# First attention: scores copied out of PSUM with their minimum, scores two units ahead of the transposes, and a buffer for the weighed maps

## The reference

```python
def diff_attn_core(q, k, v, lam):
    s = jnp.einsum('bqhcd,bkhcd->bhcqk', q.astype(jnp.float32), k.astype(jnp.float32))
    p = jax.nn.softmax(s * (1.0 / math.sqrt(HEAD_DIM)), axis=-1)
    a = p[:, :, 0] - lam * p[:, :, 1]
    return jnp.einsum('bhqk,bkhe->bqhe', a.astype(v.dtype), v)
```

## Time and profile before

| | us |
|---|---|
| median of 3 runs | 3198.42 |
| lowest and highest run | 3198.42, 3210.07 |
| the profiled execution | 3200.17 |
| its span in the trace | 3198.4 |
| TensorE (PE) busy, share | 3010.0, 94% |
| VectorE (DVE) busy, share | 1422.7, 44% |
| ScalarE (ACT) busy, share | 902.1, 28% |
| GpSimd (POOL) busy, share | 261.9, 8% |

### The profile page before, as it was taken

The page is one execution under the profiler, slowest core; times in us unless marked ns, Lnnn a source line. Parts: engine busy times, 40 slices in busy tenths (PEclk is TensorE's granted clock), DMA queues, the critical chain, the costliest instruction groups (busy, mean ns, idle before and its releaser), DMA issues. The chain is left out here.

```text
span 3198.4 us, 38018 instructions
## 1 busy us (share of the span) xinstructions
PE 3010.0 (94%) x15018; PEld 2314.2 (72%) x15018; DVE 1422.7 (44%) x2219; ACT 902.1 (28%) x1422; POOL 261.9 (8%) x278
## 2 busy tenths in 40 slices
PE   6999999899978999999999999999999988989995
PEld 4888888777734677887888888888888765764442
DVE  3646463545566466465333343333342268521113
ACT  3211121242155232223222232322233355321111
POOL 1000000001100000001000011000010145012221
PEclk8999999999989899999999999999999989989997
DMA  6323333221000166463223211223232300438995
GB/s 238 123 97 120 108 114 126 69 86 53 27 1 1 53 225 233 152 238 101 92 92 105 84 61 66 92 95 102 81 120 92 112 27 1 169 121 340 362 368 203
DMA packets 78062, 395.79 MB, mean 124 GB/s; under 512 B 17521, under 2 KB 19953, under 8 KB 51313
## 3 DMA queue, kind: packets, MB, share of 16 engines
q1 hardware_dynamic: 66416, 385.65, 32.9%
q0 software_dynamic: 11520, 8.43, 0.9%
HBM read 444.34 MB, written 16.78 MB: 144 GB/s over the span
## 5 line engine op out<-in xcount | busy, mean ns | idle before, releaser
L676 PE MATMUL ps<-h_high_ffn,weights_high_ffn 128*128 128x512 f32 (+1 forms) x1696 | 624.6, 368 | 8.4 <-issue 3.8
L677 PE MATMUL ps<-h_low_ffn,weights_high_ffn 128*128 128x512 f32 (+1 forms) x1696 | 623.5, 368 | 0.0
L678 PE MATMUL ps<-h_high_ffn,weights_low_ffn 128*128 128x512 f32 (+1 forms) x1696 | 623.0, 367 | 0.0
L676 PEld LDWEIGHTS ps<-h_high_ffn,weights_high_ffn 128*128 128x128 f32 x1696 | 320.0, 189 | 63.8 <-issue 9.2
L678 PEld LDWEIGHTS ps<-h_high_ffn,weights_low_ffn 128*128 128x128 f32 x1696 | 320.1, 189 | 53.1
L677 PEld LDWEIGHTS ps<-h_low_ffn,weights_high_ffn 128*128 128x128 f32 x1696 | 320.3, 189 | 52.7
L676 PE MATMUL ps<-hidden_high_ffn,weights_high_ffn 128*128 128x512 f32 (+1 forms) x880 | 328.2, 373 | 19.3 <-DVE weights_low_ffn L811 12.0
L760 ACT ACTIVATE weights_high_ffn<-weights 128x2048 fp32r<-128x2048 f32 (+4 forms) x160 | 243.8, 1524 | 346.6 <-PE ps L678 275.6
L811 DVE TENSOR_TENSOR weights_low_ffn<-weights,weights_high_ffn 128x2048 fp32r<-128x2048 f32 (+4 forms) x160 | 289.6, 1810 | 84.7 <-ACT weights_high_ffn L760 83.2
L677 PE MATMUL ps<-hidden_low_ffn,weights_high_ffn 128*128 128x512 f32 (+1 forms) x880 | 326.8, 371 | 0.0
L678 PE MATMUL ps<-hidden_high_ffn,weights_low_ffn 128*128 128x512 f32 (+1 forms) x880 | 326.4, 371 | 0.0
(11 more groups left out here) (438 smaller groups left out, 4563.3 us busy)
## 6 DMA issues: line engine op xcount, KB each, us to landing
weights<-in_ffn_gu SPq DMA_DIRECT2D x88, 1024.0 KB, 5.0
big<-in_w_exp_gu SPq DMA_DIRECT2D x32, 2048.0 KB, 13.0
scratch_ffn<-in_w_mod SPq DMA_DIRECT2D x35, 1536.0 KB, 6.6
weights<-in_ffn_d SPq DMA_DIRECT2D x24, 768.0 KB, 4.3
weights<-in_w_in SPq DMA_DIRECT2D x16, 1024.0 KB, 4.9
weights<-in_ffn_d SPq DMA_DIRECT2D x24, 640.0 KB, 3.9
weights<-in_w_exp_dn SPq DMA_DIRECT2D x15, 1024.0 KB, 18.4
hbuf<-in_w_exp_dn SPq DMA_DIRECT2D x12, 1024.0 KB, 19.2
```

What stands on the lines that cost most here:

```text
L676: pe.matmul(out, wh, xh, start=(k == 0), stop=False)
L677: pe.matmul(out, wh, xl, start=False, stop=False)
L678: mm = pe.matmul(out, wl, xh, start=False, stop=(k == n - 1))
```

## The change

Four things. The maximum becomes a `tensor_tensor_reduce`, which reads the scores from PSUM, adds a column of zeros, multiplies by -1, writes the result to `first_prob` in SBUF and takes its minimum; the exponential then reads SBUF, in place, with a scale of -1. The scores of a unit wait for this instruction of the unit before and no longer for the exponentials. TensorE's scores run two units ahead of the transposes, VectorE's copies one unit ahead of the weighing, and ScalarE copies the transposes of u - 2 before the exponentials of u. The weighed sum goes to a buffer of its own, `first_weighed` (two of 3 KB per partition), in place of `first_prob`. The sums of squares move from unit 1 to unit 3 of a head, and the output copy goes behind the weighing.

```diff
+        weighed = [placed(f"first_weighed{b}", (24 + 4 * b) * K1, [P, NT]) for b in range(2)]
@@ TensorE
                     if u > 0:
-                        pe.wait_ge(fm["exp"].sem, 2 * u)
+                        pe.wait_ge(fm["top"].sem, 2 * u)
...
-                        mm = pe.transpose(tp[:, m * P:(m + 1) * P], pr[u % 2][:, 0, m * P:(m + 1) * P], ident[:])
+                        mm = pe.transpose(tp[:, m * P:(m + 1) * P], weighed[u % 2][:, m * P:(m + 1) * P], ident[:])
...
                 scores(0)
+                scores(1)
                 for u in range(tiles):
-                    if u + 1 < tiles:
-                        scores(u + 1)
+                    if u + 2 < tiles:
+                        scores(u + 2)
                     turn(u)
                     if u >= QT and u % QT < 3:
                         values_product(u // QT - 1, u % QT)
-                    if u >= 2 * QT and u % QT == 1:
+                    if u >= 2 * QT and u % QT == 3:
                         out_sums(u // QT - 2)
@@ ScalarE
                 for u in range(tiles):
                     if u >= 2:
-                        scalar.wait_ge(fm["turned"].sem, u - 1)
+                        evacuate(u - 2)
                     for c in range(2):
                         scalar.wait_ge(fm["top"].sem, 2 * u + c + 1)
-                        scalar.activation(pr[u % 2][:, c, :], sc[:, c, 0:NT], ACT.Exp, bias=top[:, u % 2, c:c + 1],
+                        scalar.activation(pr[u % 2][:, c, :], pr[u % 2][:, c, :], ACT.Exp, bias=top[:, u % 2, c:c + 1], scale=-1.0,
                                           accum_out=total[:, c, u:u + 1]).then_inc(fm["exp"].sem, 1)
-                    if u > 0:
-                        evacuate(u - 1)
...
+                evacuate(tiles - 2)
                 evacuate(tiles - 1)
@@ VectorE
-                for u in range(tiles):
+                def negated(u):
                     for c in range(2):
                         vector.wait_ge(fm["scores"].sem, 2 * u + c + 1)
                         if u >= 2:
                             vector.wait_ge(fm["exp"].sem, 2 * (u - 2) + c + 1)
-                        vector.reduce_max(top[:, u % 2, c:c + 1], sc[:, c, 0:NT], AX_X, negate=True)\
-                            .then_inc(fm["top"].sem, 1)
-                    if u >= QT and u % QT == 3:
-                        output(u // QT - 1)
+                            vector.wait_ge(fm["differences"].sem, u - 1)
+                        vector.tensor_tensor_reduce(pr[u % 2][:, c, :], sc[:, c, 0:NT], column[:, 0:1].to_broadcast([P, NT]), -1.0, 3e38,
+                                                    ALU.add, ALU.min, top[:, u % 2, c:c + 1]).then_inc(fm["top"].sem, 1)
+
+                vector.wait_ge(fm["column"].sem, 2)
+                negated(0)
+                for u in range(tiles):
+                    if u + 1 < tiles:
+                        negated(u + 1)
                     vector.wait_ge(fm["exp"].sem, 2 * u + 2)
...
+                    if u >= 2:
+                        vector.wait_ge(fm["turned"].sem, u - 1)
-                    vector.scalar_tensor_tensor(pr[u % 2][:, 0, :], pr[u % 2][:, 1, :], weight, pr[u % 2][:, 0, :],
+                    vector.scalar_tensor_tensor(weighed[u % 2], pr[u % 2][:, 1, :], weight, pr[u % 2][:, 0, :],
                                                 ALU.mult, ALU.add).then_inc(fm["differences"].sem, 1)
+                    if u >= QT and u % QT == 3:
+                        output(u // QT - 1)
```

## The result

| | us |
|---|---|
| changed kernel, median of 4 runs | 3164.51 (3156.84 to 3172.84) |
| kernel before, median of 4 runs | 3198.42 (3195.23 to 3210.07) |
| ratio, 95% interval | 0.9889 (0.9869 to 0.9909) |
| profiled execution of the changed kernel, its span | 3165.37, 3163.6 |
| profiled execution of before, its span | 3200.17, 3198.4 |

The change makes the kernel 1.1% faster (0.9 to 1.3% by the interval): 34.8 us between the profiled executions, 33.9 between the medians, for 33.2 in the sum of the prediction. Three windows of the profile after (columns as in the earlier trace rows) are heads 1 to 7 from unit 5 to the last scores, the last values, and the first head with the start of unit 4.

A forecast was written before the change was run, and what follows sets the result against it. It took a loop of waits (scores, maxima, exponentials, next scores; 4.55 us) to bound the kernel's first attention. Gains of 3.8 (first head), 27.3 (units 4 to 31) and 2.1 (tail), 33.2 in all, took 3200.17 to 3167 us; range 3158 to 3190.

The forecast's parts named there:

- The loop: First attention: the next scores wait only for the copies of the unit before, 3.44 us a loop, formerly 4.55.
- TensorE bounds with values: Heads 1 to 7: TensorE's own work sets the pace in the three value units of each head, 4.04 us each.
- The new instruction: VectorE's negated copy of 768 score columns takes 0.90 us, 1.80 a unit, as the maxima did.
- Rival 2: Heads 1 to 7: VectorE or the loop bounds, at 1.22 us a copy and 4.15 a unit; 3176 us, chance 0.11.
- Order and buffer: Transposes go behind scores u+2, with a buffer of their own: no new wait, as weighing ends 1.5 us after the copies.
- The exponential out of SBUF: ScalarE's exponentials reading SBUF cost some 0.04 us more each, 0.07 a unit, beside 1.2 us of slack.
- The first head: Units 0 to 4: 22.62 us shrink to 18.6 to 18.9, scores 1 and 2 at half clock; gain 3.8.
- The clock: Heads 1 to 7: TensorE runs at 2.4 GHz throughout, where the granted clock averaged 0.93 before.
- rivals 1 and 4: Rival 1: the clock dips as now, 14% of the time at half; 3178 us, chance 0.13. Rival 4 has its own line.
- rival 4: Heads 1 to 7 slower: half clock 40% of the time breaks even, from 63% kernel 0.5% worse; 75% gives 3233; chance 0.05.
- The tail: Last first maximum to last values loses 1.0 us; last values at full clock gain 3.1; net gain 2.1.
- rival 3: Whole kernel: no change, the gain given back by later transfers or the clock elsewhere; 3197 us, chance 0.09.

The follow-up runs named there:

- the two loads: Changed kernel with an extra 256-column VectorE addition, or two extra small TensorE matmuls, in units with values: 27 periods in 105.59 and 116.6 us.
- the TensorE load: Changed kernel with two useless 128-column matmuls behind the values in every unit that carries them: 27 periods in 116.6 us, units of 4.60.
- the split on GpSimd: Changed kernel with the low half of w_o's first slab made by GpSimd instead of VectorE: unit 0 to unit 4 in 20.3 us for 15.8.
- the fillers: Kernel before with useless small matmuls in TensorE's gaps: stage 181.9 us for 190.6, ratio 0.9995 (0.9979 to 1.0011).

## Why the prediction was right

**The loop.** Forecast 1.59 + 1.80 + 0.05 = 3.44, measured 3.49. That its release decides is shown by the wait put back (5.09 in every kind of unit).

**TensorE bounds with values.** Forecast 4.04 from the rows of one unit, measured 4.02; shown by the two loads. A head takes 3 x 4.02 + 3.49 = 15.55, forecast 15.6. The sum over units 4 to 31 came out 0.8 us above the forecast (105.6 for 104.8) for one reason: the forecast took full clock throughout, and one group of scores ran at half (1.4 us).

**The new instruction.** Forecast 0.90, measured 0.88 from start to start, accumulator read hidden: the extrapolation from 256 and 512 columns (0.87) was the better row, and the operand of stride zero adds nothing that shows. Rival 2 fell.

**Order and buffer.** Priced at no new wait, and none came: the transposes start 1.49 us behind the scores, 1.50 before. The 0.33 us of idle in their row was 0.35 before and is that of the weight loads: the matmuls of the scores fill it (939.88 + 1.56 = 941.44, the transposes start at 941.37). So the prediction read a third of a microsecond of idle into TensorE's 1.50 that is hardly there, and its sign of being wrong, transposes that wait more than 0.3 us, was set below a value that the old kernel had too. The sum, taken from start to start, isn't touched. What the kernel would lose without them was not in the prediction; it is 17 us each by their experiments.

**The exponential out of SBUF** takes 924 ns instead of 897 for the 768 columns:

```profile
L1450 ACT ACTIVATE first_prob<-first_prob,top 128x768 f32<-128x768 f32 x64 | 58.9, 924 | 7.7 <-DVE top L1502 7.7
```

27 ns are less than the 35 between the two functions of the earlier trace rows. They are also less than the 43 ns estimated from the page of the Trainium skill that the prediction cites (VectorE: DVE Perf Modes, "The TRN2 errata — SBUF-src ops pay a fixed extra latency per instruction"). It is off the path either way.

**The first head was mis-sized:** 3.8 forecast, 6.8 measured. The step that failed is the assumption that scores 1 and 2 run at half clock, as scores 0 and 1 did before. They ran at full clock (units of 3.49). The execution with the TensorE load, whose edit does not touch this head, shows the other case: units of 4.86, 4.86, 3.49, 5.35, 18.56 us in all, which is the forecast 18.6. Nor does the idling just before decide it: after the same 1.93 us of it, scores 2 ran at full clock in the changed kernel and at half with the split on GpSimd:

```profile
883.58 1.56 PE L1337 MATMUL ps<-K,Q 64*128 64x512 f32 x8 [1.93 <-DVE top L1502]
...
885.67 2.93 PE L1337 MATMUL ps<-K,Q 64*128 64x512 f32 x8 [1.93 <-DVE top L1508]
```

Of the seven executions that share these units four had them at full clock. So this term is 3.8 or 6.8 from execution to execution, and the 3 us above the forecast are the luck of the one that was profiled.

**The clock.** Full in heads 1 to 7, as taken, but for one group of scores (895.91); rivals 1 and 4 fell. Of the 35.2 us of the stage's gain the dips explain some 9 to 10, by the fillers in the kernel before. Of the 26.5 between unit 4 and unit 31 the dips are 5.9 (132.1 to 126.2), and the 20.6 from there to 105.6 are the change itself, with the old loop at 4.57 us at full clock; 4.8 of them hang on the move of the sums, by the run with the sums put back. In rival 4 the 63% and the 40% are not of one kind: by its own formula heads 1 to 7 alone cost the 16 us from some 59% on.

**The tail** came out at -1.0 and +2.9. The second depends on the profile of before that is taken: by the other two it is 3.0 and 1.5. Nothing was given back later, so rival 3 fell too. That the totals lie so close, 34.8 us for 33.2, is in part chance: the first head gave 3.0 more than forecast, the other terms 1.0 less, and outside the stage the two executions differ by up to 2.6 us either way.

## What to carry to other kernels

When no engine is full, write down the loop through the one buffer that is not doubled (here the scores in PSUM) and ask which work can leave it: here the copy out of it took the place of a reduction, cost no more (two in 1.84 us for 1.82), and took 1.9 us of another engine off the loop. The release paid only with the order and the buffer that go with it; with any one of the three missing, little over a third of the gain or none was left. Then sum the new bound per kind of unit, since a mean hides that the sums of squares cost 0.95 us in one kind and nothing in another.

## What the hardware showed unexpectedly

GpSimd's subtraction over 2048 columns took 4.52 us and held up a VectorE instruction of one column with two SBUF inputs for 2.3 of them, though it left alone a copy from PSUM and a reciprocal with one input (890.39, its usual 0.16 us) beside it. A pair of 128-column matmuls behind the values took 0.58 us to the next scores, where their passes sum to 0.43. From the last pass of scores to the first transpose are 0.31 us, where such passes of 256 columns start 0.21 apart. So about 0.1 us goes where TensorE passes from one group of products to the next; whether it is the change of the product or the semaphore between the groups was not tested.

On the clock, the fillers held the granted clock at 1.00 in heads 1 to 7 of the kernel before, and shortened its stage by 8.7 us in the trace, and the median of ten runs did not move. A gain in one stage of one trace, even where it is explained to a tenth of a microsecond, needs the runs beside it.
